# Six matmuls of a weight block, ordered by PSUM bank instead of by pass

## The reference

```
h   = rms_norm(x);  z = h @ w_in                        # 2048 x 2880
q_abs, q_pe, kv_c, k_pe, u, v = projections of z        # w_q_up, w_uk, norms, rope, gelu
o   = latent attention (prompt: causal; samples: paged cache of 2048 positions)
cm  = u * (tril(w_spatial) v + b)
x  += concat(rms_norm(attn), rms_norm(cm)) @ w_out      # 2048 x 2048
x  += softmax(q k_mem) v_mem @ w_mem_o                  # 4 heads, 256 memory tokens
x  += square(relu(rms_norm(x) @ w_ffn_up)) @ w_ffn_down # 2048 x 8192, 8192 x 2048
y   = rms_norm(x)
```

## Time and profile before

| | |
|---|---|
| three runs | 2732.52, 2746.53, 2756.98 us (median 2746.53) |
| span of the profiled execution | 2727.6 us |
| TensorE matmuls busy | 2575.2 us, 94% of the span, 19084 matmuls |
| TensorE weight loads busy | 2402.3 us, 88%, 19084 loads |
| VectorE, ScalarE, GpSimd busy | 34%, 23%, 34% |
| mean granted TensorE clock | 0.975 of full |

### The profile page before, as it was taken

How to read it: one execution, slowest core, us unless ns; L and a number is a source line. 1 busy time by engine, 2 the same in 40 slices (tenths; PEclk the granted TensorE clock), 3 DMA queues, 4 the chain that set the end, 5 groups by cost and what they waited for, 6 DMA issues and landing times.

```text
span 2727.6 us, 48074 instructions
## 1 busy us (share of the span) xinstructions
PE 2575.2 (94%) x19084; PEld 2402.3 (88%) x19084; DVE 937.0 (34%) x1260; ACT 633.8 (23%) x855; POOL 919.2 (34%) x380
## 2 busy tenths in 40 slices
PE   7999878999989996999999999999999999999996
PEld 7999867444479995899999999999999999999996
DVE  5200497555443344652122131131131221221356
ACT  5111431222221132132122121121221221221221
POOL 2433432000014441233433434344343433434342
PEclk9999989899989998999999999999999999999998
DMA  5222232455432224122222222222222222222222
GB/s 220 85 85 92 93 121 70 146 155 170 145 133 87 85 78 154 40 77 92 85 86 91 85 92 85 89 88 85 92 85 91 86 86 91 85 92 85 88 89 88
DMA packets 100269, 270.68 MB, mean 99 GB/s; under 512 B 11810, under 2 KB 48707, under 8 KB 99075
## 3 DMA queue, kind: packets, MB, share of 16 engines
q1 hardware_dynamic: 92160, 243.57, 26.8%
q10 hardware_dynamic: 8066, 26.53, 2.6%
HBM read 263.72 MB, written 6.33 MB: 99 GB/s over the span
## 4 chain that ended last, share of the span: by engine, by line
PE 59%; issue 29%; POOL 8%; DVE 3%; ACT 1%; ACTq 0%; POOLq 0%; DVEq 0%
PE psum L1200 58%; POOL hl L344 8%; DVE square L1040 1%; DVE square_sum L1042 1%; DVE x L1037 0%; PE psum L1523 0%; DVE x L1187 0%; ACTq L603 0%; PE psum L1564 0%; ACT mem_probs L621 0%; PE psum L1502 0%; DVE mem_probs L1115 0%; PE psum L1537 0%; DVE head_max L1100 0%; DVE rstd_x L703 0%
## 5 line engine op out<-in xcount | busy, mean ns | idle before, releaser
L344 POOL TENSOR_TENSOR hl<-raw,hl 128x1024 fp32r<-128x1024 f32 x376 | 919.0, 2445 | 1777.5 <-ACT hl L651 913.1
L1200 PE MATMUL psum<-xg,hl 128*128 128x272 f32 x10272 | 1301.4, 289 | 33.5 <-DVE xg L698 20.3
L1200 PEld LDWEIGHTS psum<-xg,hl 128*128 128x128 f32 x10272 | 1297.5, 190 | 36.4 <-POOL hl L344 22.4
L1200 PE MATMUL psum<-ffn_hidden,hl 128*128 128x272 f32 x6144 | 765.9, 287 | 0.0
L1200 PEld LDWEIGHTS psum<-ffn_hidden,hl 128*128 128x128 f32 x6144 | 765.1, 188 | 0.0
L651 ACT CAST hl<-raw 128x1024 fp32r<-128x1024 f32 x254 | 267.7, 1054 | 1209.0 <-PE psum L1200 1209.0
L1175 DVE TENSOR_TENSOR x<-x,psum 128x544 f32 x112 | 80.9, 722 | 561.1 <-PE psum L1200 561.1
L1160 DVE SCALAR_TENSOR_TENSOR square<-psum,rstd_x 128x544 f32<-128x544 f32 x64 | 46.4, 725 | 486.2 <-PE psum L1200 486.2
L1164 DVE TENSOR_SCALAR ffn_hidden<-square 128x544 f32 x64 | 132.4, 2069 | 60.9 <-ACT square L660 60.9
L373 ACT CAST hl<-raw 128x1024 fp32r<-128x1024 f32 x64 | 67.4, 1053 | 318.6 <-PE psum L1200 318.6
L366 ACT CAST hl<-raw 128x1024 fp32r<-128x1024 f32 x58 | 60.6, 1048 | 188.6 <-PE psum L1200 136.6
(11 more groups left out here) (218 smaller groups left out, 1344.7 us busy)
## 6 DMA issues: line engine op xcount, KB each, us to landing
raw<-in_w_stream SPq DMA_DIRECT2D x376, 512.0 KB, 3.3
page_cols<-in_pool_t SPq DMA_DIRECT2D x128, 192.0 KB, 3.6
page_rows<-in_pool_n SPq DMA_DIRECT2D x128, 128.0 KB, 2.4
x<-in_x_t ACTq DMA_DIRECT2D x4, 1088.0 KB, 12.3
out<-x SPq DMA_DIRECT2D x8, 544.0 KB, 2.7
cache_k_sb<-in_mem_k_t ACTq DMA_DIRECT2D x4, 1024.0 KB, 13.2
cache_v_sb<-in_mem_v_p ACTq DMA_DIRECT2D x1, 4096.0 KB, 19.2
x<-in_x_t ACTq DMA_DIRECT2D x1, 4080.0 KB, 14.1
```

Source lines behind the costliest of these rows:

```text
L344: nc.gpsimd.tensor_tensor(HL[s % 2][:, 1, :, :], RAW[:, s, :, :], HL[s % 2][:, 0, :, :].bitcast(F32), ALU.subtract).then_inc(w_lo, 1)
L1200: last = mm(PSUM[:, s + half, 0:HALF], HL[slot][:, wp, blk, :], src[:, xp, k, HALF * half:HALF * (half + 1)], start=start and n == 0, stop ...
```

## The change

Inside `tile_block` the two loops are exchanged. The six matmuls, their operands and the number of weight loads are the same; what differs is the order of five of them.

```
--- before.py
+++ after.py
@@ -1195,8 +1195,8 @@
             def tile_block(g, slot, blk, src, k, start, stop):
 
                 s = first_bank(g)
-                for n, (wp, xp) in enumerate(PASSES):
-                    for half in range(2):
+                for half in range(2):
+                    for n, (wp, xp) in enumerate(PASSES):
                         last = mm(PSUM[:, s + half, 0:HALF], HL[slot][:, wp, blk, :],
                                   src[:, xp, k, HALF * half:HALF * (half + 1)],
                                   start=start and n == 0, stop=stop and n == 2)
```

## The result

The changed kernel takes 2753.4 us (median of 20 runs, 2748.6 to 2756.9); the kernel before, run beside it, 2745.3 us (20 runs, 2726.5 to 2757.0). The ratio of the runs is 1.0043, 95% interval 1.0026 to 1.0060 (the quotient of the two medians alone is 1.0029): slower by 0.4%. That is within the 1% that was called no change and within the range, but clear of no change at all. The two spreads say more than the medians. Before covers 30 us; after covers 8 us, at the upper end of the same range. No run of the changed kernel is as fast as the faster half of before.

A forecast was written before the change was run, and what follows sets the result against it. TensorE's back-to-back matmuls were taken as the bound, 17088 of them at an unchanged extra. Profiled span 2727.6 + 0 us, with the three runs' median 18.9 us above it, gave 2746.5 us, range 2705 to 2787 us.

The forecast's parts named there:

- What bounds the kernel, and where a cost would show: TensorE's matmuls in `tile_block` run without waits; any change must show in the 11.1 ns extra between one and the next.
- I take zero, by `mem_k`'s second piece: Change in extra per `tile_block` matmul set to zero, since that 256-wide, one-bank piece also shows 11.1 ns over its columns.
- the three new things: In each block: following matmuls write the same bank, weights change at other places, token half changes once instead of five times.
- the third thing: The token half changes once in a block of `tile_block`, not five times; no separate price.
- The last sentence of the prediction: Possible unpriced cause: token start addresses, multiples of 1024 bytes in `mem_k` but 1088 in `tile_block`; no size given.
- C, the rhythm settles elsewhere: Feed-forward matmuls settle at the input projection's 126.1 ns: 21 us more, 2767 us; chance 0.2.
- Rival A: Extra shrinks to 6.6 ns, as in `mem_k`'s first piece, by staying in one bank: 77 us less, 2670 us; chance 0.12.
- Rival B: Matmuls following into the same bank, places 2, 3, 5, 6, pay: 31 us, 2777 us, or 77 us, 2823 us; chance 0.17.
- Rival D: The change does nothing because the build restores the order or merges loads; same time as the forecast; chance 0.01.
- What would show it: Signs in feed-forward runs of 768 matmuls: 95.6 us apart if right, 92.1 for A, 96.9 or more B, 96.9 C.

The follow-up runs named there:

- the second execution of before: The kernel before run and profiled once more, unchanged: median 2739.9 us, ratio 1.0008; the profiled execution spans 2752.3 us.
- the run with banks alone: Kernel before with three results in a row to each bank, weights and tokens ordered as before: 2735.5 us, ratio 0.9991.
- the second 256 + 288 kernel: Kernel before with token parts of 256 and 288 instead of 272 twice, and the changed kernel's loop order: 2720.0 us, ratio 0.9934.

## Why the prediction was right or wrong

**What bounds the kernel, and where a cost would show: right.** The part of the difference that belongs to the change sits in the distance between matmuls, no wait came in, and 12288 matmuls by 1.67 ns are 20.5 of the 27.5 us between the two profiled executions. One reading was short without effect: 22.6 us follow the feed-forward part, of which the prediction named 18, and they are 22.6 us after as well.

**The step that failed** is "I take zero, by `mem_k`'s second piece". In the medians of the runs this term is not 0 but 8.1 us, 0.47 ns for each of the 17088 matmuls; by the ratio, 0.43% or 0.69 ns. The prediction named the three new things rightly and then priced all of them by one row, that has only two: `mem_k` has the changed kernel's order of weights and never leaves its bank, and on banks and weights it was right: neither costs anything that the runs resolve (ratios 0.9991 and 1.0006). But it has no second half, and all its token slices start a multiple of 1024 bytes apart. It could say nothing on the third thing, the order of the tokens, which made the whole effect: 126.1 ns in every stage instead of a draw between 124.4 and 126.1. The row had a warning of its own: its two pieces, 113.3 and 117.7 ns for the same code, lie further apart than anything that the change did. The last sentence of the prediction saw this difference and gave it no number.

**The base was misread, too.** The distances of before were read as fixed to the stages. They differ from execution to execution, and the profiled one had the smallest of the four for the largest stage. So it is partly luck that the forecast came within 0.3% of the measured median: it was the middle one of three runs that lay between 2732 and 2757 us, and the term added to it was wrong. "C, the rhythm settles elsewhere" had the right mechanism and the right value, 126.1 ns, at a chance of 0.2. Its price was mis-sized, 2767 us for 2753.4, because 21 us, counted from 124.4 ns, were added to a median that lies 19 us above the execution with 124.4 ns and so holds a large part of them already (an inference from the spans given with the second execution of before). Counted against the profiled span it comes nearer: 2727.6 + 20.5 = 2748 us, and 2755.1 was seen, 7 us more.

**Rival A** had a wrong cause: staying in one bank does not shrink the extra, as the run with banks alone shows: 124.4 to 126.1 ns. **Rival B** was refuted by the same run; following on in a bank at places 2, 3, 5 and 6 costs nothing that it resolves. **Rival D** is refuted: the spacing and the spread of the runs changed, so the order reaches the chip.

**What would show it** was sound in one respect: it gave 96.9 us for 768 matmuls to B and C alike, and named an order with one part of the change alone as what tells them apart, and the run with banks alone did. It failed in another: it took 95.6 us as the mark of the kernel before, and a second execution of that kernel, unchanged, shows 96.85.

**What stays open** is why a slice's start matters at all. The runs show two positions, 64 bytes apart, at 123.3 and 125.3 ns, and combinations at 123.9 to 126.1 ns; no rule for them was found, and the gain of the changed order with 256 and 288 tokens is measured, not explained. What decides which distance an execution draws was not tried either.

## What to carry to other kernels

When matmuls follow one another without a wait and each loads its weights, the time between their starts is the kernel's time, and its last per cent can hang on where the moving slices start and in which order they follow: before judging a loop order, try it with slice starts moved by 64 bytes, since the same exchange cost 0.4% here with starts 1088 bytes apart, nothing that the runs resolve with 1024 bytes at equal widths, and gained 0.4% with 1024 bytes and a 256 + 288 split. Profile the unchanged kernel twice before reading a distance out of one execution as a constant, and compare the spread of runs as well as the medians: here a narrow spread at the upper end of a wide one was the first sign of the mechanism. Price a new order only by rows that share every operand's pattern with it, the moving one included.

## What the runs showed of the hardware that was not expected

- Distances between matmuls of 128 x 128 weights and 272 columns at full clock came in steps here. One and the same program, the kernel before, had 124.4, 125.0, 125.6 and 126.1 ns in different stages and executions, 6.7 ns apart in twelve matmuls, and kept 124.4 in one execution and 126.1 in another through the feed-forward part's 12288 matmuls.
- The start of the moving slice counts: 123.3 ns and, 64 bytes on, 125.3 ns, with nothing else changed; 2708.6 and 2742.9 us.
- The order of the PSUM banks does not: with three results in a row to one bank instead of in turn to two, the distances are again 124.4 to 126.1 ns and the runs spread from 2727 to 2753 us, ratio 0.9991 (0.9964 to 1.0019).
- An instruction of VectorE that reads 544 columns across the border of two banks (the sum of the residual and PSUM) took 722 ns in the second 256 + 288 kernel (112 of them), as much as the one that reads twice 272 in the kernel before.
